# Modulation sums inside the first MLP: row gate, split operands, one operation per step

## The reference, cut to what matters

```python
c_act = jax.nn.silu(c)
for i in range(DEPTH):                       # DEPTH = 2
    mod = c_act @ ada_w[i] + ada_b[i]        # 1024 x 6144, six parts of 1024
    shift_t, scale_t, gate_t, shift_c, scale_c, gate_c = [
        m[:, None, :] for m in jnp.split(mod, 6, axis=-1)]
    h = rmsnorm(x, norm_g[i, 0]) * (1.0 + scale_t) + shift_t
    ...
    x = x + gate_t * y
    h = rmsnorm(x, norm_g[i, 1]) * (1.0 + scale_c) + shift_c
    y = jnp.square(jax.nn.relu(h @ mlp_w1[i])) @ mlp_w2[i]
    x = x + gate_c * y
```

## Time and profile before

| | |
|---|---|
| median of 3 runs | 1410.97 us (1410.11 to 1411.58) |
| the profiled execution, its own time | 1412.19 us |
| its span | 1410.4 us |
| mean granted clock of TensorE in it | 0.989 |
| busy: PE / PEld | 1353.2 us (96%) / 1188.1 us (84%) |
| busy: DVE / ACT / POOL | 960.2 us (68%) / 666.9 us (47%) / 78.7 us (6%) |
| chain that ended last, by engine | PE 83%, DVE 8%, ACT 3%, issue 2%, DMA 2% |

### The profile page before, as it was taken

The page is one execution under the profiler, slowest core; times in us unless marked ns, Lnnn a source line. Parts: engine busy times, 40 slices in busy tenths (PEclk is TensorE's granted clock), DMA queues, the critical chain, the costliest instruction groups (busy, mean ns, idle before and its releaser), DMA issues.

```text
span 1410.4 us, 20016 instructions
## 1 busy us (share of the span) xinstructions
PE 1353.2 (96%) x8376; PEld 1188.1 (84%) x8376; DVE 960.2 (68%) x1205; ACT 666.9 (47%) x875; POOL 78.7 (6%) x148
## 2 busy tenths in 40 slices
PE   6899999999999899999899999999999999999997
PEld 1797789998787789998798878999998986999996
DVE  4697787776697876655784445686777545686774
ACT  1553364444456564444534453654545446654542
POOL 1111011110010200000000010000000000000000
PEclk9999999999999999999999999999999999999999
DMA  9787278887393447555265435355553541455530
GB/s 375 272 343 268 90 260 309 297 294 267 122 360 136 161 162 260 209 184 192 102 239 182 176 120 181 148 209 181 190 194 123 214 145 59 151 209 181 188 139 30
DMA packets 46105, 279.41 MB, mean 198 GB/s; under 512 B 5200, under 2 KB 5200, under 8 KB 18880
## 3 DMA queue, kind: packets, MB, share of 16 engines
q1 hardware_dynamic: 33264, 231.57, 44.6%
q0 software_dynamic: 12752, 46.57, 8.8%
HBM read 277.07 MB, written 1.05 MB: 197 GB/s over the span
## 4 chain that ended last, share of the span: by engine, by line
PE 83%; DVE 8%; ACT 3%; issue 2%; DMA 2%; POOL 0%; SPq 0%; POOLq 0%; ACTq 0%; DVEq 0%
PE ps L1658 32%; PE ps L1784 11%; PE ps L1786 11%; PE ps L1785 11%; PE ps L1720 4%; PE ps L1690 3%; DMA ada<-in_ada_w 2%; DVE w_lo L1007 1%; PE ps L2018 1%; DVE acc L1019 1%; PE ps L1846 1%; PE ps L1819 1%; PE ps L1751 1%; ACT w_hi L607 1%; DVE h_lo L1075 1%
## 5 line engine op out<-in xcount | busy, mean ns | idle before, releaser
L1007 DVE TENSOR_TENSOR w_lo<-raw,w_hi 128x2048 fp32r<-128x2048 f32 x210 | 479.4, 2288 | 176.1 <-ACT w_hi L607 175.4
L607 ACT ACTIVATE w_hi<-raw 128x2048 fp32r<-128x2048 f32 x210 | 400.4, 1911 | 203.1 <-PE ps L1658 154.9
L1784 PE MATMUL ps<-h_hi,w_hi 128*128 128x256 f32 x1344 | 381.8, 284 | 1.9 <-ACT m_r L785 1.9
L1786 PE MATMUL ps<-h_hi,w_lo 128*128 128x256 f32 x1344 | 380.3, 283 | 0.0
L1785 PE MATMUL ps<-h_lo,w_hi 128*128 128x256 f32 x1344 | 380.3, 283 | 0.0
L1784 PEld LDWEIGHTS ps<-h_hi,w_hi 128*128 128x128 f32 x1344 | 256.3, 191 | 4.1 <-ACT m_r L785 2.3
L1785 PEld LDWEIGHTS ps<-h_lo,w_hi 128*128 128x128 f32 x1344 | 256.3, 191 | 1.9 <-issue 0.2
L1786 PEld LDWEIGHTS ps<-h_hi,w_lo 128*128 128x128 f32 x1344 | 256.3, 191 | 0.0
L1557 DVE SCALAR_TENSOR_TENSOR f_cv<-ps,cols,f_cv 128x254 f32<-128x254 f32 (+1 forms) x176 | 76.7, 477 | 71.2 <-ACT f_cv L920 69.7
L1658 PE MATMUL ps<-w_hi,hid_hi 128*128 128x512 f32 x368 | 114.5, 392 | 0.0
L1658 PE MATMUL ps<-w_hi,hid_lo 128*128 128x512 f32 x368 | 114.3, 392 | 0.0
(11 more groups left out here) (293 smaller groups left out, 1695.6 us busy)
## 6 DMA issues: line engine op xcount, KB each, us to landing
raw<-in_stream SPq DMA_DIRECT2D x210, 1024.0 KB, 4.8
ada<-in_ada_w POOLq DMA_DIRECT2D x80, 512.0 KB, 5.9
ada<-in_ada_w SPq DMA_DIRECT2D x8, 512.0 KB, 12.6
raw<-in_ada_w SPq DMA_DIRECT2D x8, 512.0 KB, 15.8
row<-in_gate_b POOLq DMA_DIRECT2D x3, 512.0 KB, 3.8
x<-in_x SPq DMA_DIRECT2D x1, 1024.0 KB, 9.7
retc<-in_retc POOLq DMA_DIRECT2D x1, 1024.0 KB, 5.0
out<-xn SPq DMA_DIRECT2D x2, 512.0 KB, 2.7
```

The source lines that it names most:

```text
L607: act.activation(w_hi[:, s, :], raw[:, s, :], ACT.Copy).then_inc(hi_done[s], 1)
L1007: dve.tensor_tensor(w_lo[:, s, :], raw[:, s, :], w_hi[:, s, :].bitcast(f32), ALU.subtract)\
L1784: pe.matmul(out, wh, h_hi[:, kt, :], start=kt == 0, stop=False)
L1786: last = pe.matmul(out, wl, h_hi[:, kt, :], start=False, stop=kt == KT - 1)
```

## The change: what it does

- Part 5 becomes a fourth `row_gate` (its number 1): PE at the head of unit 5 in place of `sum_part(5)`, DVE in unit 5. `make_diag`, `gate` and `gate_row` go, and POOL loads one bias row more, behind the eight loads of part 5 and a wait for x of the stage before.
- Parts 6, 7, 8: the steps now come four in a unit, in units 5 and 6, 8 and 9, 11 and 12. In units 7, 10, 13 ACT writes `acc_hi` (rounded, 1024 columns) and DVE `acc_lo = acc - acc_hi`. PE sums them at the head of units 8, 11, 14 (`sum_negative`): 16 float32r products with two columns of minus ones. `finish_negative` subtracts.
- A step is one operation of 1024 columns wherever there are steps; `ada_half` goes.
- The one rounded constant block `maskr` gets two blocks more, written by the same ACT operation.

```diff
-ADA_IN_MLP = {u: (2, 3, 3)[(u - 1) % 3] for u in range(1, 13)}
+ADA_IN_MLP = {1: (5, 0, 2), 2: (5, 2, 3), 3: (5, 5, 3)}
+ADA_IN_MLP.update({u: ((u + 13) // 3, 4 * ((u - 5) % 3), 4) for u in (5, 6, 8, 9, 11, 12)})
-ROW_GATES = (GA_T, 6 + GA_T, 6 + GA_C)
+ROW_GATES = (GA_T, GA_C, 6 + GA_T, 6 + GA_C)
...
 # POOL
-            for s in range(5 * KT, 9 * KT + ADA_RING):
+            for s in range(5 * KT, 6 * KT):
+                ada_load(s)
+            pool.wait_ge(x_done, X_GLA)
+            gate_bias(1)
+            for s in range(6 * KT, 9 * KT + ADA_RING):
                 ada_load(s)
             norm(2)
...
 # ACT, mlp
-                    if layer == 0 and u == UNITS - 1:
-                        gate_row()
+                    if layer == 0 and u in (7, 10, 13):
+                        act.wait_ge(ada_step, (u + 14) // 3 * KT)
+                        act.activation(acc_hi[:, :], acc[:, :], ACT.Copy).then_inc(acc_high, 1)
                     if u < 2:
                         hi(c0 + 4 + u)
                     else:
                         hi(mlp_up(c0, u) + 5)
...
 # DVE, add_step
-                for half, done in ((slice(0, 512), ada_half), (slice(512, D), ada_step)):
-                    rows, ck = place[:, half], csil[:, k:k + 1]
...
+                if k == 0:
+                    dve.tensor_scalar(acc[:, :], place, csil[:, 0:1], None, ALU.mult).then_inc(ada_step, inc)
+                else:
+                    dve.wait_ge(ada_step, s)
+                    dve.scalar_tensor_tensor(acc[:, :], place, csil[:, k:k + 1], acc[:, :], ALU.mult, ALU.add)\
+                        .then_inc(ada_step, inc)
...
 # DVE, mlp
                         lo(mlp_up(c0, u) + 5)
+                    if layer == 0 and u == 5:
+                        row_gate(1)
+                    if layer == 0 and u in (8, 11, 14):
+                        finish_negative((u + 10) // 3, 6)
                     if layer == 0 and u in ADA_IN_MLP:
-                        if u > 1 and u % 3 == 1:
-                            finish_part(part, 6)
-                            part = part + 1
-                        steps(part * KT + (0, 2, 5)[(u - 1) % 3], ADA_IN_MLP[u])
-                    if layer == 0 and u == 13:
-                        finish_part(part, 6)
-                        make_diag(GA_C)
+                        part, first, n = ADA_IN_MLP[u]
+                        steps(part * KT + first, n)
+                    if layer == 0 and u in (7, 10, 13):
+                        dve.wait_ge(acc_high, (u - 4) // 3)
+                        dve.tensor_tensor(acc_lo[:, :], acc[:, :], acc_hi[:, :].bitcast(f32), ALU.subtract)\
+                            .then_inc(acc_rest, 1)
...
 # PE
+            def sum_negative(p, bank, n):
+
+                pe.wait_ge(acc_rest, n)
+                pe.wait_ge(mod_done, p)
+                for j in range(KT):
+                    for part in (acc_hi, acc_lo):
+                        last = pe.matmul(ps[:, bank, 2 * j:2 * j + 2], part[:, j * P:(j + 1) * P], maskr[:, 6 * P:6 * P + 2],
+                                         start=part is acc_hi, stop=part is acc_lo)
+                last.then_inc(ada_mm, 1)
...
                 for u in range(2, UNITS):
-                    if layer == 0 and u >= 5 and u % 3 == 2:
-                        sum_part(u // 3 + 4, 6)
+                    if layer == 0 and u == 5:
+                        row_gate(1)
+                    if layer == 0 and u in (8, 11, 14):
+                        sum_negative((u + 10) // 3, 6, (u - 5) // 3)
...
                     cols_chunk(mlp_up(c0, u), 4 + u % 2, (lambda: turn(layer, 1)) if u == 2 else None)
-                    if layer == 0 and u == UNITS - 1:
-                        pe.wait_ge(mod_done, 9)
-                        gate()
                     down(u - 2)
```

More of the change, by code:

```diff
@@ L150, in build @@
         row = sb("row", [P, D])
+        acc_offset = nc.sbuf_base
         acc = sb("acc", [P, D])
@@ L158, in build @@
         csil = sb("csil", [P, KT])
-        maskr = sb("maskr", [P, 5 * P], f32r)
+        maskr = sb("maskr", [P, 7 * P], f32r)
         gng = sb("gng", [P, GDV])
@@ L211, in build @@
         f_p = at("f_p", 6144, [2, 2, T])
-        diag = at("diag", 9216, [KT, P])
+        acc_hi = at("acc_hi", 11264, [D], f32r)
+        acc_lo = nc.alloc_sbuf_tensor_at("acc_lo", [P, D], f32r, offset=acc_offset)
         fc = at("fc", 10240, [2, TT, 256])
@@ L289, in build @@
         y_dve = sem("y_dve")
-        diag_done = sem("diag_done")
-        gate_mm = sem("gate_mm")
-        gate_done = sem("gate_done")
+        acc_high = sem("acc_high")
+        acc_rest = sem("acc_rest")
         gate_in = sem("gate_in")
@@ L558, in _ @@
             norm(1)
[L560 removed]
+            for s in range(5 * KT, 6 * KT):
[3 more added lines that the diff above has]
+            for s in range(6 * KT, 9 * KT + ADA_RING):
                 ada_load(s)
             norm(2)
[L564 removed]
+            gate_bias(2)
             for s in range(9 * KT + ADA_RING, 10 * KT + 6 + ADA_RING):
@@ L573, in _ @@
             norm(3)
-            gate_bias(2)
+            gate_bias(3)
             for s in range(11 * KT + ADA_RING, ADA_STEPS):
@@ L695, in read_y @@
                         .then_inc(y_act, 1)
[L697 to L703, removed]
             act.wait_ge(cols_in, 16)
@@ L720, in _ @@
             act.activation(maskr[:, P:4 * P], shp[:, S_CAUS:S_CAUS + 3 * P], ACT.Copy)
-            act.activation(maskr[:, 4 * P:5 * P], shp[:, S_SBM:S_SBM + P], ACT.Copy).then_inc(mask_done, 1)
+            act.activation(maskr[:, 4 * P:7 * P], shp[:, S_SBM:S_SBM + 3 * P], ACT.Copy).then_inc(mask_done, 1)
             act.wait_ge(ada_pe, KT)
@@ L1083, in split_stage, with finish_negative @@
                                       ALU.subtract).then_inc(hl_done, 1)
[L1085 to L1090, removed]
+            def finish_negative(p, bank):
+                dve.wait_ge(ada_mm, p + 1)
+                dve.tensor_tensor(mod[:, p * KT:(p + 1) * KT], cols[:, COL_ADAB + p * KT:COL_ADAB + (p + 1) * KT],
+                                  ps[:, bank, 0:2 * KT].rearrange("p (k o) -> p k o", o=2)[:, :, 0], ALU.subtract)\
+                    .then_inc(mod_done, 1)
             def row_gate(n):
@@ L1310, in mlp @@
                 B = UNITS * layer
-                part = 5
                 for u in range(UNITS):
@@ L1338, in mlp @@
                     if layer == 1 and u == UNITS - 2:
-                        row_gate(2)
+                        row_gate(3)
             mlp(0, C_M0)
             norm_scale(2, 6 + SC_T)
-            dve.wait_ge(gate_done, 1)
+            dve.wait_ge(mod_done, GA_C + 1)
             boundary(add_gated, Y_M0, 2, TR_N2, C_DQ)
@@ L1451, in _ @@
             lo(C_DO + 5)
-            row_gate(1)
+            row_gate(2)
             dve.wait_ge(mod_done, 6 + GA_T + 1)
```

7 lines of the change are left out of this document (removed).

## The result

The changed kernel takes 1439.74 us (median of 4 runs, 1439.53 to 1445.29) against 1411.28 us (4 runs on the same chip, 1410.11 to 1412.09): 1.0212 of the time before, 95% interval 1.0186 to 1.0237 (the two medians alone give 1.0202; one of the four runs took 1445.29). It is slower, by 28.5 us; the forecast was 28.0. The profiled execution has a span of 1437.7 us against 1410.4, 27.3 more.

A forecast was written before the change was run, and what follows sets the result against it. PE was taken as the bound, busy in all 155.00 us of the first MLP's bulk. Terms 21.6 + 9.3 - 1.7 - 0.95 - 0.3 gave +28.0 us on the median 1410.97, so 1439.0, range 1431 to 1445.

The forecast's parts named there:

- three waits for `acc_lo`: PE at the heads of units 8, 11, 14 idles 7.2 us each until DVE's subtraction ends: +21.6 us.
- lower clock behind them: After each idle gap PE runs the sum and up product partly at 1.2 GHz: 3.1 us each, +9.3.
- one sum less, gate product moved: On PE sum_part(5) goes, -1.7 us; gate goes and row_gate(1) of the same form comes in unit 5, 0.
- end of the MLP: Without ACT's gate_row the work PE waits for before its transposes comes earlier: -0.95 us.
- sums 6 to 8 in float32r: On PE the 16 float32r weight loads per sum cost what the float32 ones did: 0.
- elsewhere: In the attention stages one-operation steps save 0.05 us each and shorten PE's wait for part 3: -0.3 us.
- The new wait: Before each sum, the chain hid_hi, acc_hi, w_hi, w_lo, subtraction starts when PE reaches the sum; 7.2 us, none hidden.
- DVE ready first by 0.9: In unit 7 DVE is ready for the last w_lo before ACT's w_hi, ACT ending last by some 0.9 us.
- Cheap sums: Rival: float32r weight loads in the sums go twice as fast, 2.5 us less in total, 1436.5; chance 0.10.
- no wait: Rival: acc_lo is written in time and the sums stay hidden; only savings, -3.0, 1408.0 us; chance 0.03.
- a wait with the clock at 1.00: Rival: PE waits for acc_lo but its clock holds; +18.7, 1429.7 us; chance 0.06.
- DVE would be the later one: Rival: dependent steps take 1.6 us, not 1.3, so each wait is longer; about 1444.5 us; chance 0.06.

The follow-up runs named there:

- e5: The changed kernel with 30 unread float32r products of 512 columns on PE ahead of each wait for acc_lo; 1430.02 us, ratio 1.0133.
- e1: The changed kernel with plain sums: parts 6 to 8 summed from acc in float32 as before, no acc_hi or acc_lo; 1410.27 us, ratio 0.9991.
- e4: The changed kernel with the split moved forward on ACT and DVE and the sum behind the up product; 1409.99 us, ratio 0.9993.
- e6: The changed kernel with DVE's subtraction moved ahead of the unit's second w_lo, nothing else moved; 1429.74 us, ratio 1.0131.
- e2: The changed kernel with PE's sum behind the up product of units 8, 11, 14, the split where it was; 1418.78 us, ratio 1.0056.
- e3: The changed kernel with acc_hi ahead of ACT's wait for the down product and DVE's subtraction behind m_sq, sum unmoved; 1418.31 us, ratio 1.0046.
- e10: e2 with five unread products of 512 columns in each gap ahead of the sum; 1413.94 us, ratio 1.0016.
- e9: The kernel of e1 run once more, unchanged, beside the kernel before; 1409.56 us, ratio 0.9989.
- e7: The kernel before with its steps in one operation of 1024 columns, nothing else; 1410.93 us, ratio 1.0002.
- e8: The kernel of e1 with its steps in two operations again; 1410.12 us, ratio 0.9989.

## Why the prediction was right

Forecast and measurement, term by term, in the order of the sum:

| term | forecast | measured |
|---|---|---|
| three waits for `acc_lo` | +21.6 (7.2 each) | +21.3 (7.09 each), e5: +21.6 |
| lower clock behind them | +9.3 (3.1 each) | +10.8 (3.5, 4.2, 3.1), e5: 10.5 |
| one sum less, gate product moved | -1.7 | together -2.8 |
| end of the MLP | -0.95 | (e1: 182.4 to 179.6) |
| sums 6 to 8 in float32r | 0 | 0 (e4: 1.70 us a sum) |
| elsewhere | -0.3 | -2.0 in these two traces |

The first four give 29.3, the difference of the two MLPs; with the rest 27.3, the difference of the spans; the medians differ by 28.5. The forecast for the MLP alone was 28.3. That the whole came within 0.5 us is partly luck: the clock was put 1.5 us too low, and the rest moved 1.7 us further the other way.

- **The new wait.** Right in its links, its length and its cause. The step that carried it was to follow the wait back until it met work that PE issues just ahead of the waiting product; from there on nothing hides. e6 took `w_hi` and `w_lo`, 4.1 us, out of the chain, and the gap fell by 3.0 to 3.4 us, as the subtraction then stands behind `hid_lo`; e4 took the whole chain off PE's path and the gap was gone.
- **The clock.** Right in kind, low by 0.5 a gap. In the sum of 16 products I took +1.4 from the earlier trace rows, measured were 3.44 - 1.70 = 1.7; behind it I took 1.7 of loss, measured 1.4 to 2.5. The forecast put it all down to the idle time, and e5 shows that filling the gap brings it back. But one of its three rows was misread: ahead of the gap that ends at 42.69, PE runs a sum of 16 narrow products and, without a pause, 16 more of one column, and the clock falls among these, before the gap begins (from 0.14 x 2.2/0.5 = 0.6 us ahead of 39.4). A longer row of narrow products lowered the clock there with no gap ahead of it:

```profile
37.23 2.19 PE L1856 MATMUL ps<-shp,srow 1*128 1x1 f32 x16
37.20:39.40 2.20, 2.20 (x17) 2.12 (x17) 0.17 (x1) 1.12 (x1) 0.68 (x2) 0.86 1.00 417
```

- **DVE ready first by 0.9.** It was, by 0.74. I had counted 1.3 for a step in one operation; four of them take 5.37 us up to the next operation, 1.34 each. The margin was thinner than I took it for, but ACT stayed last.
- **Cheap sums.** The estimate from the Trainium skill (TensorE: Matmul & The Clock Gate, Weight-path perf modes), 2.5 us less if float32r loads counted among those that are read in parallel, does not hold here: e4 shows 1.70 us for 16 products of float32r, each with its load, the same as in float32. The rival is out.
- **The end of the MLP.** With plain sums the last relu comes 19.2 us ahead of the first product behind the MLP, against 21.9 before (179.6 and 182.4, less the relu distances): 2.7, the gate product of unit 15 and the copy on ACT together. The forecast had 1.7 in unit 5 and 0.95 here; in unit 5 only 0.08 is gained (relu 4 to 5 takes 12.95 for 13.03), as `row_gate(1)` fills the place of the sum, and the time comes back where the gate product stood. PE's wait of 1.01 us before the transposes is no longer among its waits in the changed kernel and in e1.
- **Elsewhere.** The first relu came at 187.9 against 189.5, inside the scatter of 4 us, and behind the MLP 0.4 us are gained; neither is shown to come from the change. The 0.05 us a step that the forecast put into this term is not there: a dependent step got slower, as shown below.

The two rivals that have no wait, or a wait with the clock at 1.00, are ruled out by the changed kernel's own trace; e4 and e5 show what each of them would have looked like. That DVE would be the later one did not come about.

## What to carry to other kernels

Where PE never idles, moving a preparation to other engines is not free because those have slack: follow the last link of the new operand back, and if it starts from work that PE issues just ahead of the place where it is used, the whole chain is idle time. Place the use behind the next long product, and the preparation ahead of waits that it does not need; both were necessary here (e2 and e3 each still lost 7 us, e4 nothing). And price a gap with the clock behind it: a row of the same work at the lower level shows it. A short gap counts too where narrow products follow it.

## What was not expected

- **A gap of 1.2 us with narrow products behind it can cost over 3 us more.** In e2 three equal gaps of 1.2 us cost 1.5, 4.7 and 3.1 us; filled with five products (e10) the clock stayed at 1.00. In the MLP the kernel before runs the same number of narrow products with no gap and stays at 1.00. In e9 0.45 us ahead of such a sum was enough. The Trainium skill (TensorE: Matmul & The Clock Gate, HAM oscillation — how this bites in real kernels) warns of idle gaps longer than those of e2 and e3; the measurement decides, and these traces show the lower clock behind gaps of 1.2 to 1.7 us too, with the narrow products behind them.
- **One operation of 1024 columns is a little slower than two of 512 here.** The groups of the changed kernel (busy us, mean ns | idle before):

```profile
L1014 DVE SCALAR_TENSOR_TENSOR acc<-ada,csil,acc 128x1024 f32<-128x1024 f32 x73 | 93.6, 1283 | 14.8 <-DMA ada<-in_ada_w 8.9 <-issue 0.6
L790 ACT ACTIVATE acc_hi<-acc 128x1024 fp32r<-128x1024 f32 x3 | 3.1, 1040 | 0.0
```

  One step lasts 1.283 us, but each waits for the one before: the four of unit 6 span 5.45 us, so their starts are (5.45 - 1.283)/3 = 1.39 apart. In two halves each waits for a half that ended an operation ago; six of them span 4.06 us, so their starts are (4.06 - 0.745)/5 = 0.663 apart though each lasts 0.745, and a step takes 1.33. (The 0.677 and 1.354 in e7's expectation are 4.06/6 and twice that, which count the end of the last one too.) So a step in one operation is 0.06 us slower, not faster; with DVE off PE's path that changes nothing, as e7 and e8 show.
- **The start of the program scatters by 4 us** over executions with equal instructions, while a unit of the MLP without a sum agrees to 0.02 us. For a difference of 0.1% the distance between two marks in the trace says more than the whole time.
